# Narrower constant products on half the rows, and three more pairs of them between the projections

## The chip, the cores and the metric

The kernel runs on one core of a Trainium2 chip. The metric is the device time of one launch in microseconds (us). The time before is the median of three launches; a fourth launch was taken with the hardware profiler on, and all rows of the trace come from it.

## What is computed

Two layers on one sequence of 256 tokens with model width 2048, all in float32. The first is a hybrid layer: a norm, one wide input projection (`w_in`), a gated causal convolution, a diagonal state-space scan, two output projections that are mixed by gates, and a projection `w_o` with a residual. The second is a layer with dilated attention and an RWKV time mix side by side, an output projection, and a gated feed-forward of width 5632. Cut to the lines that matter here:

```python
m = sigmoid(ga) * ya + sigmoid(gb) * yb          # first layer: the mixture
x = rmsnorm(x + m @ w_o, final_g)                # "wo"
proj = rms_norm(x, norm1_g) @ w_in_2             # "lora", "rkv", "qkv"
mixed = concat([attention(q, k, v), rwkv(z)])
h = x + mixed @ w_out_2                          # "wouta" (attention half), "woutb" (rwkv half)
gate, up = split(rms_norm(h, norm2_g) @ w_gate_up_2)   # "ffn"
out = rms_norm(h + (silu(gate) * up) @ w_down_2, final_g_2)   # "down"
```

Batch 1, depth 1. Nothing in the change touches a value that reaches the output.

## The kernel before

Activations are kept transposed, features on the 128 partitions and the 256 tokens along the free dimension. All weights stream from memory once, as units of 128x1024 float32 (eight blocks of 128 input features for 128 output features), through a ring of four buffers. For each unit SyncE starts the load into `w_raw`, ScalarE writes the rounded copy `w_hi` (line 495), VectorE writes the remainder `w_lo` (line 976), and TensorE multiplies. The helper `unit` (lines 1680 to 1693) does it: for each of the eight blocks, three products of 128x256 into one PSUM bank, `w_hi` by the high part of the activations (line 1690), `w_hi` by the low part (line 1691) and `w_lo` by the high part (line 1692). A "column" is one block of 128 output features: two units, 48 products, where the input is 2048 wide. In the stages `glu`, `outb`, `wouta` and `woutb` a block is one unit, 24 products.

The stages follow one another in the order of `STREAM`: `u`, `zb`, `conv` (with the scan's products between its columns), `gb`, `outa`, `glu`, `outb`, `wo`, `lora`, `rkv`, `qkv` (with attention between its columns), the RWKV chunks with `wouta` between them, `woutb`, `ffn`, `down`. TensorE's program is written by hand in this order, part of it straight and part in loops (`Fori`); it waits on semaphores for `w_lo`, for a free bank, and at the start of a stage for its input. Four PSUM banks (`ps_main`) go round for the columns. The others (`ps_aux`) are used by the scan, the heads and the norms.

`half_rows` (lines 1712 to 1714) multiplies constants: twice a 64-row part of the identity (64x128) by the same rows of a ramp (64x256), each into a bank of `ps_aux` of its own. Its results are never read. It is called five times: at the start of `gb` (573 us in the trace), after the 14th block of `rkv` (1020), and after the second, third and fourth columns of `ffn` (1486, 1492, 1499). In the trace one call is four products, since a float32 product is recorded as two.

Around the new calls: `wo` runs over 16 columns in a loop of four turns, and the first column waits block by block for the mixture (`m_ready`); after each column VectorE adds the residual, makes the two parts of the next input and sums the squares (lines 1250 to 1258). `norm_total` (line 1814) sums those over partitions after half a column of `lora`. `woutb` runs over 16 blocks of one unit, with VectorE adding each into the residual (line 1604).

Of the kernel before, what the change touches and what calls it, by code (L numbers as in the profile page):

```python
# [16 lines left out]
L = 256  # L17
# [11 lines left out]
CH = 64  # L29
# [97 lines left out]
def hybrid_kernel(nc, wmain, wdown, bst_dram, cst_dram, par_dram, const_dram, x_dram, lora_dram,  # L127
                  gup_dram, bias_dram, out_dram):
    ctx = ExitStack()
    with ctx:  # L130
# [7 lines left out]
        def sem(name):  # L138
            return ctx.enter_context(nc.semaphore(name))
# [27 lines left out]
        def hilo(name, kb, blocks):  # L167
            t = wk(name, kb, [2, blocks, L], F32R)
            return t, t[:, 0, :, :], t[:, 1, :, :]
# [35 lines left out]
        ms, mh, ml = hilo("ms", 0, KB)  # L205
# [43 lines left out]
        aux = ctx.enter_context(nc.psum_tensor("ps_aux", [P, 4, 512], F32))  # L249
# [7 lines left out]
        def cst(name):  # L257
            c, w = CCOLS[name]
            return const[:, c:c + w]
# [25 lines left out]
        ya_ready, gelu_ready, yb_ready, glu_out, yo_ready, m_ready = (  # L285
            sem("ya_ready"), sem("gelu_ready"), sem("yb_ready"), sem("glu_out"), sem("yo_ready"), sem("m_ready"))
# [27 lines left out]
        def hrow(h):  # L314
            return slice(64 * h, 64 * h + 64)
# [1360 lines left out]
        def _(pe):  # L1676
# [3 lines left out]
            def unit(n, out, xs_, kb0, kbs, first, last, split=None):  # L1680

                s = n.c % RING
                high, low = xs_ if isinstance(xs_, tuple) else (xs_[:, 0, :, :], xs_[:, 1, :, :])
                pe.wait_ge(lo_ready, n.v(1))
                for kk in range(kbs):
                    w = slice(kk * P, (kk + 1) * P)
                    k = kb0 + kk
                    if split and k % (split[2:] or (1,))[0] == 0:
                        pe.wait_ge(split[0], split[1] + k // (split[2:] or (1,))[0] + 1)
                    nc.tensor.matmul(out, whi[:, s, w], high[:, k, :], start=(first and kk == 0), stop=False)  # L1690
                    nc.tensor.matmul(out, whi[:, s, w], low[:, k, :], start=False, stop=False)  # L1691
                    ins = nc.tensor.matmul(out, wlo[:, s, w], high[:, k, :], start=False, stop=(last and kk == kbs - 1))  # L1692
                ins.then_inc(unit_used, 1)

            def bank(g):
                return main[:, g.c % 4, 0:L]

            def free(g):
                if g.i is not None or g.c >= 4:
                    pe.wait_ge(bank_free[g.c % 4], g.turns(4))  # L1700

            def whole(n, out, xs_, split=None):

                unit(n, out, xs_, 0, 8, True, False, split)
                unit(n + 1, out, xs_, 8, 8, False, True, split)

            def column(n, g, xs_, split=None):

                free(g)
                whole(n, bank(g), xs_, split)  # L1710

            def half_rows(b):
                for h in range(2):
                    nc.tensor.matmul(aux[:, b + h, 0:L], cst("ident")[hrow(h), :], cst("iota")[hrow(h), :], start=True, stop=True)

            n0, g0 = UNIT0["u"], BLOCK0["u"]
            free(At(g0))
# [20 lines left out]
            n0, g0 = UNIT0["zb"], BLOCK0["zb"]  # L1738
# [30 lines left out]
            n0, g0 = UNIT0["conv"], BLOCK0["conv"]  # L1769
            with pe.Fori(0, SB) as i:  # L1770
                for p, kind in enumerate(KINDS):
# [11 lines left out]
                    else:  # L1783
                        column(n, At(g0 + conv_bank(p), 8, i), xs)
            n0, g0 = UNIT0["gb"], BLOCK0["gb"]
            half_rows(0)
            with pe.Fori(0, 4) as i:
                for b in range(4):
# [3 lines left out]
            n0, g0 = UNIT0["outa"], BLOCK0["outa"]  # L1792
# [4 lines left out]
            n0, g0 = UNIT0["glu"], BLOCK0["glu"]  # L1797
# [3 lines left out]
            n0, g0 = UNIT0["outb"], BLOCK0["outb"]  # L1801
# [2 lines left out]
                    free(At(g0 + b, 4, i))  # L1804
                    unit(At(n0 + b, 4, i), bank(At(g0 + b, 4, i)), yos, 0, 8, True, True, (yo_ready, 0) if b == 0 else None)
            n0, g0 = UNIT0["wo"], BLOCK0["wo"]
            with pe.Fori(0, 4) as i:
                for b in range(4):
                    column(At(n0 + 2 * b, 8, i), At(g0 + b, 4, i), ms, (m_ready, 0) if b == 0 else None)

            def norm_total(n, w):

# [4 lines left out]
            n0, g0 = UNIT0["lora"], BLOCK0["lora"]  # L1817
# [8 lines left out]
            n0, g0 = UNIT0["rkv"], BLOCK0["rkv"]  # L1826
# [25 lines left out]
            for b in range(12, 14):  # L1852
                column(At(n0 + 2 * b), At(g0 + b), ns)
            pe.wait_ge(kk_clamped, 1)
            half_rows(0)
            for b in range(14, 16):
                column(At(n0 + 2 * b), At(g0 + b), ns)
# [46 lines left out]
            n0 = UNIT0["qkv"]  # L1904
# [88 lines left out]
            n0 = UNIT0["wouta"]  # L1993
# [17 lines left out]
            for i in range(NCH):  # L2011
# [110 lines left out]
                if not last:  # L2122
                    wout(2)
                    for j in range(8):
                        for h in range(2):
                            ins = nc.tensor.matmul(S[hrow(h), j * CH:(j + 1) * CH], bkt[:, j, hrow(h)], st[:, j, h, :],
                                                   start=True, stop=True)
# [14 lines left out]
            n0, g0 = UNIT0["woutb"], BLOCK0["woutb"]  # L2142
            for b in range(KB):
                if b < 4 and (g0 + b) % 4 < 2:
                    pe.wait_ge(wa_free[(g0 + b) % 4], KB // 2)
                free(At(g0 + b))
                unit(At(n0 + b), bank(At(g0 + b)), (rwh, rwl), 0, 8, True, True)
            n0, g0 = UNIT0["ffn"], BLOCK0["ffn"]
            for b in range(4):
                column(At(n0 + 2 * b), At(g0 + b), x3s, (in_ready, KB) if b == 0 else None)  # L2150
                if b == 0:
                    norm_total(3, L)
                else:
                    half_rows(0)
# [3 lines left out]
            n0, g0 = UNIT0["down"], BLOCK0["down"]  # L2158
# [189 lines left out]
```

## Time and profile before

| | us |
|---|---|
| median of three launches | 2205.65 |
| the three launches | 2205.65, 2211.58, 2204.10 |
| the profiled launch | 2210.97 |
| its span, first to last instruction | 2209.3 |
| TensorE busy (matmul) | 2157.9 |
| VectorE busy | 1571.0 |
| ScalarE busy | 1042.1 |

Times of day in the rows are microseconds from the start of the span. A record of a wide product is longer than the distance to the next one, since products are pipelined and their ends are modelled; the pace is read from the starts. In the source view a row has the shortest, median and longest duration in ns, then the first and the last start. Some records of products are missing from a trace.

### The profile page before, as it was taken

The page shows a single profiled execution, that of the slowest core. Times are in us where ns is not written, and L with a number is a line of the kernel's source. Part 1 is how long each engine was busy: PE and PEld are TensorE (multiplying, and loading weights), DVE is VectorE, ACT ScalarE, POOL GpSimd, SP SyncE. Part 2 cuts the span into 40 slices and gives each one's busy share as a digit, 9 for nine tenths or more (in the row PEclk, how much of TensorE's full clock was granted, in tenths as well). Part 3 has the DMA queues.
Part 4 walks back from the last instruction along what each step waited for, and adds up shares of the span by engine and source line. Part 5 has one row for each costly group of instructions (what it writes and reads, how often), then busy time and mean ns, then how long its engine had stood idle before and what let it go on. Part 6 is the DMA issues. An engine that isn't in the chain of part 4 may idle for free.

```text
span 2209.3 us, 51676 instructions
## 1 busy us (share of the span) xinstructions
PE 2157.9 (98%) x20592; PEld 2100.5 (95%) x20592; DVE 1571.0 (71%) x2060; ACT 1042.1 (47%) x1357; POOL 267.1 (12%) x178
## 2 busy tenths in 40 slices
PE   7999999999999999999999999899999999999997
PEld 7999999999999989999999888799999999999997
DVE  7889999999645667768877767676666666654544
ACT  6544444444554444466344454564444444434443
POOL 0354544444200000100011000000000000000000
PEclk9999999999999999999999999999999999999999
DMA  7555555555665556555655111255566566666664
GB/s 260 185 172 181 181 179 180 190 184 183 196 195 195 193 191 199 180 178 172 209 185 189 62 50 41 70 181 190 190 192 195 193 194 194 190 186 196 189 191 141
DMA packets 107106, 387.84 MB, mean 176 GB/s; under 512 B 12032, under 2 KB 12160, under 8 KB 106752
## 3 DMA queue, kind: packets, MB, share of 16 engines
q1 hardware_dynamic: 104400, 375.44, 52.5%
q0 software_dynamic: 2176, 9.78, 1.3%
q8 instruction: 74, 1.21, 0.2%
q10 hardware_dynamic: 432, 1.21, 0.1%
q14 instruction: 24, 0.20, 0.0%
HBM read 384.29 MB, written 2.10 MB: 175 GB/s over the span
## 4 chain that ended last, share of the span: by engine, by line
PE 79%; DVE 14%; issue 4%; ACT 2%; DMA 0%; DVEq 0%; SPq 0%; ACTq 0%
PE ps_main L1690 23%; PE ps_main L1692 23%; PE ps_main L1691 23%; DVE w_lo L976 6%; PE ps_aux L1931 2%; ACT w_hi L495 1%; PE ps_main L1931 1%; DVE m L1135 1%; DVE m L1136 1%; PE ps_main L2004 1%; DVE acc L1142 1%; PE ps_aux L1952 1%; DMA w_raw<-wmain 0%; DVE g_scan L1145 0%; PE ps_main L2005 0%
## 5 line engine op out<-in xcount | busy, mean ns | idle before, releaser
L976 DVE TENSOR_TENSOR w_lo<-w_raw,w_hi 128x1024 fp32r<-128x1024 f32 x718 | 918.3, 1296 | 419.7 <-ACT w_hi L495 413.8
L495 ACT ACTIVATE w_hi<-w_raw 128x1024 fp32r<-128x1024 f32 x718 | 748.5, 1048 | 700.3 <-PE ps_main L1692 656.5
L1690 PE MATMUL ps_main<-xs,w_hi 128*128 128x256 f32 x1664 | 463.4, 278 | 7.2 <-DVE w_lo L976 6.1
L1691 PE MATMUL ps_main<-xs,w_hi 128*128 128x256 f32 x1664 | 460.4, 277 | 0.0
L1692 PE MATMUL ps_main<-xs,w_lo 128*128 128x256 f32 x1664 | 460.4, 277 | 0.0
L1690 PE MATMUL ps_main<-x3s,w_hi 128*128 128x256 f32 x1408 | 389.4, 277 | 0.0
L1692 PE MATMUL ps_main<-x3s,w_lo 128*128 128x256 f32 x1408 | 388.9, 276 | 0.0
L1691 PE MATMUL ps_main<-x3s,w_hi 128*128 128x256 f32 x1408 | 388.9, 276 | 0.0
L1690 PEld LDWEIGHTS ps_main<-xs,w_hi 128*128 128x128 f32 x1664 | 312.8, 188 | 15.6 <-DVE w_lo L976 11.3
L1692 PEld LDWEIGHTS ps_main<-xs,w_lo 128*128 128x128 f32 x1664 | 312.8, 188 | 0.0
L1691 PEld LDWEIGHTS ps_main<-xs,w_hi 128*128 128x128 f32 x1664 | 312.4, 188 | 0.0
L1690 PEld LDWEIGHTS ps_main<-x3s,w_hi 128*128 128x128 f32 x1408 | 264.4, 188 | 1.0 <-issue 1.0
L1692 PEld LDWEIGHTS ps_main<-x3s,w_lo 128*128 128x128 f32 x1408 | 264.4, 188 | 0.0
L1691 PEld LDWEIGHTS ps_main<-x3s,w_hi 128*128 128x128 f32 x1408 | 264.3, 188 | 0.0
L1690 PE MATMUL ps_main<-ns,w_hi 128*128 128x256 f32 x816 | 229.2, 281 | 0.3 <-DVE w_lo L976 0.3
L1692 PE MATMUL ps_main<-ns,w_lo 128*128 128x256 f32 x816 | 226.3, 277 | 0.0
L1691 PE MATMUL ps_main<-ns,w_hi 128*128 128x256 f32 x816 | 226.2, 277 | 0.0
L1690 PE MATMUL ps_main<-act,w_hi 128*128 128x256 f32 x704 | 194.3, 276 | 0.0
L1691 PE MATMUL ps_main<-act,w_hi 128*128 128x256 f32 x704 | 194.3, 276 | 0.0
L1692 PE MATMUL ps_main<-act,w_lo 128*128 128x256 f32 x704 | 194.3, 276 | 0.0
L1690 PEld LDWEIGHTS ps_main<-ns,w_hi 128*128 128x128 f32 x816 | 153.9, 189 | 7.7 <-issue 7.2
L1691 PEld LDWEIGHTS ps_main<-ns,w_hi 128*128 128x128 f32 x816 | 153.3, 188 | 0.2 <-issue 0.2
(422 smaller groups left out, 3771.5 us busy)
## 6 DMA issues: line engine op xcount, KB each, us to landing
w_raw<-wmain SPq DMA_DIRECT2D x622, 512.0 KB, 3.4
w_raw<-wdown SPq DMA_DIRECT2D x80, 512.0 KB, 3.7
w_raw<-wdown SPq DMA_DIRECT2D x16, 256.0 KB, 2.7
bias<-bias POOLq DMA_DIRECT2D x8, 384.0 KB, 3.4
x_res<-xt POOLq DMA_DIRECT2D x4, 512.0 KB, 7.0
out<-x_res SPq DMA_DIRECT2D x3, 512.0 KB, 2.8
x_first<-xt SPq DMA_DIRECT2D x2, 512.0 KB, 7.0
x_first<-xt ACTq DMA_DIRECT2D x2, 512.0 KB, 9.6
```

The costliest lines, as they stand in the source:

```text
L495: nc.scalar.activation(whi[:, s, 0:width], raw[:, s, 0:width], ACT.Copy).then_inc(hi_ready, 1)
L976: V.tensor_tensor(wlo[:, s, 0:width], raw[:, s, 0:width], whi[:, s, 0:width].bitcast(F32), ALU.subtract)\
L1135: V.tensor_tensor(m1[:, :, :], bu, cb, ALU.mult)
L1136: V.tensor_tensor(m2[:, :, :], bu, sb_, ALU.mult).then_inc(bu_used, 1)
L1142: link(V.tensor_tensor(g[:, 1, :], m1[:, 1, :], m2[:, 0, :], ALU.subtract))
L1690: nc.tensor.matmul(out, whi[:, s, w], high[:, k, :], start=(first and kk == 0), stop=False)
L1691: nc.tensor.matmul(out, whi[:, s, w], low[:, k, :], start=False, stop=False)
L1692: ins = nc.tensor.matmul(out, wlo[:, s, w], high[:, k, :], start=False, stop=(last and kk == kbs - 1))
L1931: ins = nc.tensor.matmul(banks[h][hrow(h), j * CH:(j + 1) * CH], *fn(j, h), start=True, stop=True)
L1952: ins = nc.tensor.matmul(banks[:, j // 4, (j % 4) * P:(j % 4 + 1) * P], bkc[hrow(h), j, :, :].rearrange("p a n -> p (a n)"), abr[hrow(h), ...
L2004: nc.tensor.matmul(out, whi[:, s, w], atth[:, k, :], start=(k == 0), stop=False)
```

## The change

`half_rows` multiplies only the first 64 columns of the ramp, in all its calls. It is called three times more: after the first and the second column of `wo`, and after the second block of `woutb`. For that the first four columns of `wo` are written out and the loop has three turns; the wait for the mixture stays with the first column alone.

```diff
             def half_rows(b):
                 for h in range(2):
-                    nc.tensor.matmul(aux[:, b + h, 0:L], cst("ident")[hrow(h), :], cst("iota")[hrow(h), :], start=True, stop=True)
+                    nc.tensor.matmul(aux[:, b + h, 0:CH], cst("ident")[hrow(h), :], cst("iota")[hrow(h), 0:CH],
+                                     start=True, stop=True)
...
             n0, g0 = UNIT0["wo"], BLOCK0["wo"]
-            with pe.Fori(0, 4) as i:
+            for b in range(4):
+                column(At(n0 + 2 * b), At(g0 + b), ms, (m_ready, 0) if b == 0 else None)
+                if b in (0, 1):
+                    half_rows(0)
+            with pe.Fori(1, 4) as i:
                 for b in range(4):
-                    column(At(n0 + 2 * b, 8, i), At(g0 + b, 4, i), ms, (m_ready, 0) if b == 0 else None)
+                    column(At(n0 + 2 * b, 8, i), At(g0 + b, 4, i), ms)
...
                 free(At(g0 + b))
                 unit(At(n0 + b), bank(At(g0 + b)), (rwh, rwl), 0, 8, True, True)
+                if b == 1:
+                    half_rows(0)
```

`L` is 256 and `CH` is 64.

## Rows read from the trace of the kernel before

**Rows 1.** The page: TensorE's busy time, and the granted clock in 40 slices.
```profile
PE 2157.9 (98%) x20592; PEld 2100.5 (95%) x20592; DVE 1571.0 (71%) x2060; ACT 1042.1 (47%) x1357; POOL 267.1 (12%) x178
...
PEclk9999999999999999999999999999999999999999
```

**Rows 2.** Source view, line 1690: duration ns min/median/max, first and last start.
```profile
L1690 PE MATMUL ps_main<-x3s,w_hi x1408: 276/276/468, 1474.2 to 1956.2; 128*128 128x256 f32 x176
...
L1690 PE MATMUL ps_main<-act,w_hi x704: 276/276/276, 1956.5 to 2195.5; 128*128 128x256 f32 x176
...
L1690 PE MATMUL ps_main<-yas,w_hi x256: 276/276/276, 661.4 to 748.1; 128*128 128x256 f32 x128
...
L1690 PE MATMUL ps_main<-rwkv_h,w_hi x128: 277/281/388, 1428.9 to 1473.9; 128*128 128x256 f32 x128
```

**Rows 3.** Timeline of TensorE around the pair at 1486: start, duration in us.
```profile
1485.83 0.28 PE L1692 MATMUL ps_main<-x3s,w_lo 128*128 128x256 f32 x1
1486.04 0.70 PE L1714 MATMUL ps_aux<-const 64*128 64x256 f32 x4
1486.67 0.38 PE L1690 MATMUL ps_main<-x3s,w_hi 128*128 128x256 f32 x1
1486.89 0.28 PE L1691 MATMUL ps_main<-x3s,w_hi 128*128 128x256 f32 x1
```

**Rows 4.** Source view, line 1690, in the stretches before and after each pair.
```profile
L1690 PE MATMUL ps_main<-xs,w_hi x16: 281/281/384, 567.8 to 573.2; 128*128 128x256 f32 x16
...
L1690 PE MATMUL ps_main<-xs,w_hi x256: 276/276/384, 574.3 to 661.1; 128*128 128x256 f32 x128
...
L1690 PE MATMUL ps_main<-ns,w_hi x31: 281/281/281, 1008.9 to 1019.5; 128*128 128x256 f32 x31
...
L1690 PE MATMUL ps_main<-ns,w_hi x159: 276/276/281, 1021.0 to 1074.7; 128*128 128x256 f32 x159
...
L1690 PE MATMUL ps_main<-x3s,w_hi x16: 281/281/468, 1480.1 to 1485.6; 128*128 128x256 f32 x16
...
L1690 PE MATMUL ps_main<-x3s,w_hi x16: 281/281/384, 1486.7 to 1492.1; 128*128 128x256 f32 x16
...
L1690 PE MATMUL ps_main<-x3s,w_hi x15: 276/276/281, 1493.6 to 1498.4; 128*128 128x256 f32 x15
...
L1690 PE MATMUL ps_main<-x3s,w_hi x1343: 276/276/279, 1499.9 to 1956.2; 128*128 128x256 f32 x192
```

**Rows 5.** Timeline of TensorE at the attention scores, 64-row products of two widths.
```profile
1101.77 0.50 PE L1871 MATMUL ps_main<-qkv 64*128 64x128 f32 x4
1102.09 0.61 PE L1872 MATMUL ps_main<-qkv 64*128 64x256 f32 x4
1102.63 0.38 PE L1690 MATMUL ps_main<-ns,w_hi 128*128 128x256 f32 x1
```

**Rows 6.** Start of `wo`: timeline, windows (TensorE, loads, VectorE, ScalarE, GpSimd, clock), source view.
```profile
826.31 0.42 PE L1690 MATMUL ps_main<-ms,w_hi 128*128 128x256 f32 x1 [2.20 <-DVE ms L1223]
...
826.40:829.90 3.50, 3.50 (x17) 3.48 (x18) 3.10 (x5) 1.86 (x2) 0.53 (x1) 0.52 0.78 276
...
L1690 PE MATMUL ps_main<-ms,w_hi x237: 281/281/415, 829.6 to 913.1; 128*128 128x256 f32 x119
```

**Rows 7.** Timeline of VectorE at the end of the last column of `wo`.
```profile
913.80 0.42 DVE L1250 TENSOR_TENSOR x_res<-x_res,ps_main 128x256 f32 x1 [0.44 <-PE ps_main L1692]
```

**Rows 8.** TensorE in `lora`: timeline at its two waits, source view between them.
```profile
916.75 1.13 PE L1814 MATMUL ps_aux<-acc,const 128*128 128x512 f32 x2 [0.26 <-DVE tmp L1260]
...
L1690 PE MATMUL ps_main<-ns,w_hi x42: 281/281/281, 919.8 to 934.3; 128*128 128x256 f32 x42
...
935.15 0.39 PE L1690 MATMUL ps_main<-ns,w_hi 128*128 128x256 f32 x1 [0.31 <-DVE w_lo L976]
```

**Rows 9.** Timeline of VectorE at one block of `woutb`.
```profile
1468.76 0.42 DVE L1604 TENSOR_TENSOR x_res<-x_res,ps_main 128x256 f32<-128x256 f32 x1 [0.37 <-PE ps_main L1692]
```

**Rows 10.** Before the scan's `y` products at 566.79: source view, then timeline.
```profile
L1690 PE MATMUL ps_main<-xs,w_hi x23: 276/276/276, 558.9 to 566.4; 128*128 128x256 f32 x23
...
566.79 0.41 PE L1763 MATMUL ps_aux<-h_state_a,c_stage 128*32 128x256 f32 x2
```

## The prediction

> **What bounds the kernel now.** I read the page first. TensorE is busy 98% of the span and the granted clock is full in all 40 slices [rows 1], so the time is what TensorE needs for its stream of products, not a wait for another engine. Next I read the line of the main products by operand [rows 2]. Every k-step is three wide products (128x256), and their starts give the pace. `yas`: 256 records of one line in 86.7 us, so 765 products between the first and the last, 113.3 ns each. `act`: 704 records in 239.0 us, 113.3 ns again. `rwkv_h` is the same kind of product at the same clock, and its 381 steps take 45.0 us, 117.8 ns each once the first, longer step is taken off. Nothing waits there. The reader should also see the modelled length of a record: 276 ns where the pace is 113.3, 281 ns where it is 117.8. So TensorE has two paces at full clock, 4.5 ns apart, and the 276 or 281 of a stretch tells which.
>
> When does the pace change? The same line, stretch by stretch [rows 4], says that inside an undisturbed stream it does not: 281 from 1429 to 1486, 276 for all 1343 records after 1500. It changes only at an interruption. The pair of constant products (L1714) is one. The pairs at 573, 1020 and 1492 stand between a 281 and a 276 stretch, and the pair at 1486 between two 281 stretches. The fifth, at 1499, has 276 on both sides. Of four pairs met at the slow pace three turned it, and the one met at the fast pace kept it.
>
> **The cost of a pair today.** In the timeline [rows 3] the last wide start before a pair is 1485.83 and the second after it is 1486.89: 1.06 us, where two ordinary steps at 117.8 ns take 0.24. A pair costs 0.82 us, and nothing hides it, since TensorE is the bound.
>
> **64 columns in place of 256.** No row has a 64-row, 128-column weight with 64 moving columns. The nearest are the score products [rows 5]: with 128 columns the two take 0.32 us (1101.77 to 1102.09), with 256 columns 0.54 (to 1102.63). That is 0.22 us for 128 columns, so 0.33 for the 192 that go. Bounds: nothing saved, if the weight loads set the time, and at most the 0.63 us from the pair's start to the next wide one [rows 3]. I take 0.33, since the rows are two thirds of the way there. A new pair then costs 0.49 us, and the five old ones together give back 1.65 us (0 to 3.15).
>
> The Trainium skill (TensorEngine Tiling (Array Packing), Tiling Modes, Key Properties) says that a change of tiling mode drains TensorE. That speaks against this change: the drain does not shrink with the columns, and three more pairs bring three more of them. It is inside the 0.82 us of the row here, so the sum would be the same.
>
> **The two new pairs in the mixture's projection (`wo`).** It starts at 818. TensorE waits 2.20 us for `ms`, and from 826.4 to 829.9 the granted clock is 0.52, the lower level; then it is full again and the pace is 281 to the end at 913.1 [rows 6]. The column that ends near 827.5 is the first, so the first pair falls into the slow clock and costs about double, 0.98 us. Whatever pace it leaves meets another interruption when the clock rises at 829.9, so I count no gain from it. The second pair comes a column later at full clock, 0.49 us. After it 14 columns of 48 products are left: 672 x 4.5 ns = 3.02 us if it turns the pace. VectorE does not take its place: at the end of a column it waits 0.44 us for the product [rows 7], a column shortens by 48 x 4.5 ns = 0.22 us, so 0.22 us of slack stays. Late next is the sum for the norm: TensorE already waits 0.26 us for it at 916.75 [rows 8], and that grows by the 24 x 4.5 ns of the half column before it, 0.1 us given back. The projection to the low ranks behind it is slow too (281), but it ends in a wait for `w_lo` at 935.15 [rows 8] whose chain runs over VectorE and ScalarE. I count 0 there (at most 144 x 4.5 ns = 0.65 us). Writing the first four columns out and dropping the repeated waits on `m_ready` moves no work. I put it at nothing: instructions are fetched under the stream, as in the first four columns of the feed-forward, which are written out already. Without that cover it could cost a wait of some tenths.
>
> **The pair in the second half of the output projection.** It comes after 2 of 16 blocks, 0.49 us. Left: 14 x 24 = 336 products, 1.51 us. VectorE waits 0.37 us per block for the product [rows 9], a block shortens by 0.11 us, so it stays hidden. The pace would be kept into the feed-forward, whose first three columns (to the pair at 1492) are at 281 now: 144 x 4.5 ns = 0.65 us.
>
> **Sum.** Costs: -1.65 + 0.98 + 0.49 + 0.49 = +0.31 us. Gains: -3.02 + 0.10 - 1.51 - 0.65 = -5.08 us. Together -4.8 us. The profiled execution took 2210.97 us (span 2209.3), so this would be 2206.2 under the profiler. The median of the three runs, 2205.65, lies 5.3 us below the profiled time, and the three spread over 7.5 us. That is about the size of these paces, so some of those runs may have the fast pace where the profile has the slow one. If the median run is slow in the same places it becomes 2200.9. If it is fast in all of them only +0.3 is left, 2206.0. I take 2202.6, a little nearer to the first.
>
> **The rivals.**
>
> *The pace is lost after a shorter pair* (slower). Five old calls are changed too, and the largest stretches hang on them. An interruption can also turn fast into slow: the `y` products at 566.79 stand between a 276 stretch and a 281 one [rows 10]. If a pair of another length leaves the slow pace after the third call of the feed-forward, the 84 columns left of `ffn` (4032 products) and the 2112 of `down`, 6144 in all, take 4.5 ns more: +27.6 us, 2202.6 + 27.6 = 2230. If it happens at the pair of 573, the 768 + 768 + 192 products of `gb`, `outa` and `glu` are slow: +7.8 us, 2210.4. At 1020 it is the ten columns left of `rkv`, 480 products, +2.2 us. It decides from about (6.6 + 3.0) / 0.0045 = 2100 slow products on, so by itself only in the feed-forward. For it: one of four calls failed at the slow pace. Against it: three calls in a row stand before the long stretch. The chance of the 2230 case is 0.17, of the 2210 case 0.13.
>
> *The new pairs turn nothing* (no change). They cost 0.31 us net and the slow stretches stay: 2206. The Trainium skill (TensorE: Matmul & The Clock Gate, Back-to-back issue gap) gives an isolated step as columns by clock plus a fixed floor, 109.2 ns for 256 columns, with no second pace; by it no product before a stream could change its pace. The trace differs: 113.3 and 117.8 ns in the same form. For this rival is the failed call at 1486, and that the pace may already be fast in many runs. Chance 0.2.
>
> *More than forecast*: the 64-column pair costs near nothing and turns the pace every time, and the median runs are slow as the profile is. 3.15 us saved in place of 1.65, low ranks 0.65 too, and the costs of the new pairs halved (0.98): 2200.9 - 3.1 = 2197.8. Chance 0.12.
>
> The forecast itself keeps 0.38.
>
> **How the numbers follow.** A measurement of this kernel can tell about 0.3%, 6.6 us, from no change: 2199.0 to 2212.3. Faster by more: the last rival and a tail of run spread, 0.15. Slower by more: the feed-forward case 0.17, and a third of the 2210 case, 0.04: 0.21. The rest, 0.64, is within. The range takes in the third rival from 2197.5 and the 2210 case with some spread, to 2214; it leaves out the feed-forward case (0.17) and little below.
>
> **What would show it.** In the changed profile: records of 281 or 276 ns in `ms` after the second pair, in `rwkv_h` after the pair, and in the first columns of `x3s`; a start-to-start over a pair of about 0.73 us in place of 1.06; waits for `w_lo` and for the norm's sum no more than 0.1 us longer. The prediction is wrong if the `x3s` and `act` records after the third call show 281, or if the `xs` records after 574 do, or if a pair costs as much as before. It is also wrong in its reason if the time moves with these stretches unchanged.

## The result, and the profile after

The changed kernel takes 2215.16 us (median of 18 launches, 2207.19 to 2220.59), the kernel before 2207.92 us (18 launches, 2203.10 to 2214.14). The ratio is 1.0034, with a 95% interval of 1.0024 to 1.0044: slower by 7.2 us, where 3 us less was forecast. The profiled launch took 2218.19 us with a span of 2216.5, against 2210.97 and 2209.3 before, so the two traces differ by the same 7.2 us and can be compared step by step.

The source view of line 1690 over the whole of the changed kernel answers to [rows 2]. Its columns are the durations in ns (min/median/max), then the first and last start.

```profile
L1690 PE MATMUL ps_main<-xs,w_hi x1664: 275/276/389, 60.8 to 662.8; 128*128 128x256 f32 x185
L1690 PE MATMUL ps_main<-x3s,w_hi x1408: 275/276/468, 1482.4 to 1963.4; 128*128 128x256 f32 x176
L1690 PE MATMUL ps_main<-ns,w_hi x816: 275/276/682, 917.7 to 1233.3; 128*128 128x256 f32 x164
L1690 PE MATMUL ps_main<-act,w_hi x704: 275/276/277, 1963.8 to 2202.8; 128*128 128x256 f32 x176
L1690 PE MATMUL ps_main<-yas,w_hi x256: 280/281/282, 663.1 to 753.2; 128*128 128x256 f32 x128
L1690 PE MATMUL ps_main<-ms,w_hi x256: 275/276/569, 824.3 to 917.4; 128*128 128x256 f32 x128
L1690 PE MATMUL ps_main<-yos,w_hi x128: 276/281/389, 776.2 to 823.3; 128*128 128x256 f32 x128
L1690 PE MATMUL ps_main<-rwkv_h,w_hi x128: 275/276/415, 1436.6 to 1482.1; 128*128 128x256 f32 x128
```

The row to see is `yas`: 281 ns, and 90.1 us from its first start to its last, where it was 276 ns and 86.7 us [rows 2]. `ms` and `rwkv_h`, the stages of the new pairs, read 276 in place of 281. The new pairs did not bring that. The stream was at 276 ahead of all three already, as the source view shows just before the pairs at 841.0 and 1443.9 (the one at 833.4 met 276 too):

```profile
L1690 PE MATMUL ps_main<-ms,w_hi x10: 276/276/277, 837.5 to 840.6; 128*128 128x256 f32 x10
...
L1690 PE MATMUL ps_main<-rwkv_h,w_hi x6: 276/276/277, 1441.7 to 1443.4; 128*128 128x256 f32 x6
```

The first starts of these rows, set against those of the kernel before, give where the time went:

| first start of | before | after | after less before |
|---|---|---|---|
| `xs` (`zb`) | 61.9 | 60.8 | -1.1 |
| `yas` (`outa`) | 661.4 | 663.1 | +1.7 |
| `yos` (`outb`) | 770.2 | 776.2 | +6.0 |
| `ms` (`wo`) | 818.3 | 824.3 | +6.0 |
| `ns` (`lora`) | 913.5 | 917.7 | +4.2 |
| `rwkv_h` (`woutb`) | 1428.9 | 1436.6 | +7.7 |
| `x3s` (`ffn`) | 1474.2 | 1482.4 | +8.2 |
| `act` (`down`) | 1956.5 | 1963.8 | +7.3 |
| end of the span | 2209.3 | 2216.5 | +7.2 |

From the start to `yos` +7.1 us comes in `gb`, `outa` and `glu`. `outb` is slow too (`yos` reads 281) but takes the same 48.1 us as before: TensorE waits less for `w_lo` in it, 1.3 us in place of 2.2. `wo` gives back 1.8. From `lora` to `woutb` 3.5 are lost. `woutb` gives nothing (+0.5), though its pace is the fast one.

The source view of line 1690 stretch by stretch, before and after each pair, answers to [rows 4]:

```profile
L1690 PE MATMUL ps_main<-xs,w_hi x15: 281/281/282, 566.8 to 571.8; 128*128 128x256 f32 x15
...
L1690 PE MATMUL ps_main<-xs,w_hi x255: 280/281/282, 573.0 to 662.8; 128*128 128x256 f32 x128
...
L1690 PE MATMUL ps_main<-ns,w_hi x31: 281/281/282, 1012.8 to 1023.4; 128*128 128x256 f32 x31
...
L1690 PE MATMUL ps_main<-ns,w_hi x160: 280/281/389, 1024.2 to 1080.5; 128*128 128x256 f32 x160
...
L1690 PE MATMUL ps_main<-x3s,w_hi x15: 281/281/468, 1488.1 to 1493.3; 128*128 128x256 f32 x15
...
L1690 PE MATMUL ps_main<-x3s,w_hi x16: 281/281/388, 1494.4 to 1499.8; 128*128 128x256 f32 x16
...
L1690 PE MATMUL ps_main<-x3s,w_hi x16: 276/276/387, 1500.6 to 1505.9; 128*128 128x256 f32 x16
...
L1690 PE MATMUL ps_main<-x3s,w_hi x1342: 275/276/384, 1506.7 to 1962.7; 128*128 128x256 f32 x192
```

The pairs at 572 and 1024 left the slow pace, where those of 256 columns had turned it. In the feed-forward the first failed and the second worked, as before. The two failures hold 1728 + 480 products or 7.8 + 2.2 us.

Of the 3.5 us lost between `lora` and `woutb` 2.2 are these in `rkv`. The 192 products at the start of `qkv` are fast here (276 in place of 281) and give 0.9 back. That is not luck: the 64x512 products just ahead of them (at 1075 in the kernel before) turned the pace in every one of the 14 profiles, fast to slow in the ten where `rkv` ended fast and slow to fast in the four where it ended slow. So a failed pair in `rkv` costs 1.3 us net. The rest lies behind the last `ns` product, 203.3 us to the first `rwkv_h` where the kernel before takes 200.6. It is a lower clock, the second and third of the dips below; the kernel with only the old pairs narrowed, which has no dip there, takes 200.6 as well. (A dip is a short stretch at the lower clock.) The windows view shows four dips to half, of 3.4 us each (after the window come the busy times of TensorE, its loads, VectorE, ScalarE and GpSimd, then the granted clock):

```profile
833.80:837.20 3.40, 3.40 (x18) 3.40 (x17) 3.08 (x5) 0.53 (x2) 0.00 (x0) 0.50 0.70 223
...
1253.70:1257.10 3.40, 3.38 (x70) 3.40 (x72) 0.00 (x0) 1.74 (x4) 0.00 (x0) 0.50 0.03 5
1420.90:1424.30 3.40, 3.13 (x50) 2.82 (x52) 2.04 (x3) 0.00 (x0) 0.00 (x0) 0.50 0.02 5
1438.00:1441.40 3.40, 3.40 (x19) 3.40 (x18) 2.16 (x4) 0.12 (x1) 0.00 (x0) 0.50 0.31 110
```

In the dips at 833.8 and 1438 the wide products start every 213 ns in place of 113, so 3.4 us hold 16 of them and such a dip costs about 1.6 us. The kernel before has the dip at 826 [rows 6] and one in its first 25 us. The dip at 1438 and the new pair took the gain of `woutb`: at the fast pace with neither, in the kernel with only the old pairs narrowed, the stage takes 43.6 us, and 43.6 + 1.6 + 0.6 is the 45.8 us here. Ahead of those at 833.8 and 1438 TensorE had waited, 2.26 us for `ms` and 3.2 us for `rwkv_l`. These dips come and go from launch to launch, as the experiments show.

### The profile page after: what moved, and what is told of

The parts are those of the page before. It is cut to its first block, busy times and chain, and to the rows that moved or that the text cites. A ratio compares the mean times of both kernels' runs of the same rounds, so it can differ in the third digit from the quotient of the medians.

```text
span 2216.5 us, 51686 instructions
## 1 busy us (share of the span) xinstructions
PE 2164.6 (98%) x20604; PEld 2108.0 (95%) x20604; DVE 1570.9 (71%) x2060; ACT 1041.6 (47%) x1357; POOL 267.5 (12%) x178
## 4 chain that ended last, share of the span: by engine, by line
PE 79%; DVE 14%; issue 4%; ACT 2%; DMA 1%; DVEq 0%; SPq 0%; ACTq 0%
PE ps_main L1690 24%; PE ps_main L1692 23%; PE ps_main L1691 23%; DVE w_lo L976 6%; PE ps_aux L1936 2%; PE ps_main L1936 1%; ACT w_hi L495 1%; DMA w_raw<-wmain 1%; DVE m L1135 1%; DVE m L1136 1%; PE ps_main L2009 1%; DVE acc L1142 1%; PE ps_aux L1957 1%; DVE g_scan L1145 0%; PE ps_main L2010 0%
## 5 line engine op out<-in xcount | busy, mean ns | idle before, releaser
L1690 PEld LDWEIGHTS ps_main<-ns,w_hi 128*128 128x128 f32 x816 | 153.4, 188 | 7.8 <-issue 6.8
L1692 PEld LDWEIGHTS ps_main<-ns,w_lo 128*128 128x128 f32 x816 | 153.9, 189 | 0.0
```

## The experiments

Theory A: the width. A 64-column pair turns the slow pace more rarely. Theory B: the new pairs and the dips near them cost the time, and the width is harmless. Theories C (chance, the same at every width) and D (what counts is when the stream resumes) came in with the sampling.

**The width alone.** Only the first hunk of the change, no new pair.

```diff
-                    nc.tensor.matmul(aux[:, b + h, 0:L], cst("ident")[hrow(h), :], cst("iota")[hrow(h), :], start=True, stop=True)
+                    nc.tensor.matmul(aux[:, b + h, 0:w], cst("ident")[hrow(h), :], cst("iota")[hrow(h), 0:w],
+                                     start=True, stop=True)          # w = CH
```

> The kernel before with its five pairs cut to 64 columns and no new pair. Theory A (a 64-column pair rarely turns the slow pace: 1 of 4 in the changed kernel, against 3 of 4 with 256 columns): in the profile the stretches after the pairs at the start of gb and in rkv read 281 ns, gb to glu cost 1728 x 4.5 ns = 7.8 us and rkv 2.2 us, less 5 x 0.27 us for the shorter pairs: +8 to +9 us against the kernel before, a ratio near 1.004. Theory B (the new pairs and the clock dips around them made the kernel slower, the width is harmless): -1.3 us, ratio 0.9994, with 276 ns after the two pairs.

Measured: ratio 1.0037 (1.0023 to 1.0050), 2215.85 us against 2207.98. That is as much as the whole change. Line 1690 in this kernel:

```profile
L1690 PE MATMUL ps_main<-yas,w_hi x256: 281/281/281, 664.3 to 754.4; 128*128 128x256 f32 x128
L1690 PE MATMUL ps_main<-ms,w_hi x256: 276/276/419, 825.5 to 917.4; 128*128 128x256 f32 x128
...
L1690 PE MATMUL ps_main<-rwkv_h,w_hi x128: 276/276/383, 1433.8 to 1477.0; 128*128 128x256 f32 x128
```

`yas` is slow, as theory A says. There is a second reading: `ms` and `rwkv_h` read 276 with no pair in their stages. The 281 of these stages in the kernel before [rows 2, 6] was that launch's.

**The new pairs alone, at 256 columns.** The changed kernel with `0:L` in the helper.

> All eight pairs, at 256 columns. Theory A: gb and rkv are back at 276 ns, wo after its second pair and woutb after its pair at 276 too where they were 281; three pairs cost 0.8 us each (the first 1.6 in the low clock): -5.1 + 3.2 = about -2 us, ratio 0.999, never above 1.001. Theory B: as slow as the changed kernel, ratio 1.003.

Measured: ratio 1.0007 (0.9996 to 1.0019), 2208.31 us. Theory A's forecast of 2 us less did not come either, but theory B falls. `yas`, `ms` and `rwkv_h` all read 276, and still nothing is gained over the kernel before: three pairs are paid for stages that mostly run fast anyway.

**The changed kernel with two pairs wide again**, those at the start of `gb` and in `rkv`.

```diff
-            half_rows(0)
+            half_rows(0, L)          # at the start of gb, and after the 14th column of rkv
```

> The changed kernel with only the pairs at the start of gb and in rkv back at 256 columns, the other six at 64. Theory A: both stretches at 276 ns in most launches, 8 to 10 us under the changed kernel: about -3 us against the kernel before, ratio 0.998 to 1.000. Theory B: no better than the changed kernel, 1.003.

Measured: ratio 1.0012 (1.0003 to 1.0021), 2210.35 us. Two of the eight pairs take most of the 1.0034 away. The 0.998 to 1.000 that was expected is missed. Its interval overlaps that of the version with all pairs wide. In its profile the second narrow pair of `wo`, at 834.9, failed too, so all of `wo` was slow behind it.

**No pair at `gb`.** The kernel before without the first call.

```diff
             n0, g0 = UNIT0["gb"], BLOCK0["gb"]
-            half_rows(0)
```

> The kernel before without the pair at the start of gb. If the products of gb, outa and glu keep the pace that the scan's last products left, they read 281 ns and the launch is 7.8 - 0.8 = 7 us longer, ratio 1.003. If a stream falls back to 113.3 ns by itself within it, or if the two paces are only a matter of the record, -0.8 us, ratio 0.9996.

Measured: ratio 1.0026 (1.0014 to 1.0038), 2213.78 us. The stream keeps the pace that the scan's last products left it, 281 ns for all of `gb`, `outa` and `glu`:

```profile
L1690 PE MATMUL ps_main<-xs,w_hi x270: 281/281/281, 566.8 to 661.8; 128*128 128x256 f32 x135
L1690 PE MATMUL ps_main<-yas,w_hi x256: 281/281/281, 662.2 to 752.3; 128*128 128x256 f32 x128
```

So one pair of 0.82 us was worth 5.8 us net, and the narrow one, which fails here, is worth nothing.

**Sampling the pair.** In `outa`, where columns run without a wait, each column is followed either by the scan's kind of constant products (met at 276 they left 281, in 32 of 32 samples; met at 281 they left 276, in 8 of 8) or by a pair. The pair's width is the only thing that differs between the kernels.

```diff
-            with pe.Fori(0, 4) as i:
-                for b in range(4):
-                    column(At(n0 + 2 * b, 8, i), At(g0 + b, 4, i), yas)
+            def flip():
+                for part in range(2):
+                    for t in range(TPB):
+                        nc.tensor.matmul(aux[32 * t:32 * t + 32, 2, 0:L], cst("ident")[:, 32 * t:32 * t + 32], cst("iota"),
+                                         start=(part == 0), stop=(part == 1), tile_position=(0, 32 * t))
+            for b in range(16):
+                column(At(n0 + 2 * b), At(g0 + b), yas)
+                if b % 2:
+                    half_rows(0)
+                else:
+                    flip()
```

> The kernel before with all pairs at 64 columns, and in outa, after each of its 16 columns in turn, either the scan's kind of constant products (eight of 128x32 weights by 256 columns, which turned 276 into 281 in the scan) or a pair. Each column reads 276 or 281 ns and so tells what the product before it did. Theory A (the width of a pair decides how often it turns the slow pace): at 64 columns fewer than half of the pairs met at 281 give 276; none met at 276 gives 281. Rival C (chance alone, the same for every width): about the same share as with 256 columns.

> The same with pairs of 128 columns. Theory A in its simple form (more columns, more turns) puts the share between those of 64 and 256 columns. If what counts is the moment at which the stream resumes and not the width as such (theory D), the share need not lie between. A pair should take about 0.1 us more than with 64.

> The same with pairs of 192 columns. Theory A: a share near that of 256 columns. Theory D: any share, as the resume falls 0.1 us earlier than with 256.

> The same with pairs of 256 columns, as in the kernel before. Theory A and D: nearly every pair met at 281 gives 276 (10 of 11 in the profiles so far). Rival C: no more than with 64 columns.

One launch each, 2224.99, 2225.03, 2224.24 and 2222.15 us beside 2210.46 (the sampling itself costs some 12 us). Four columns in a row with 256 columns, line 1690: after the scan's kind, after a pair, and so on.

```profile
L1690 PE MATMUL ps_main<-yas,w_hi x15: 281/281/281, 666.8 to 671.8; 128*128 128x256 f32 x15
...
L1690 PE MATMUL ps_main<-yas,w_hi x15: 276/276/281, 673.3 to 678.1; 128*128 128x256 f32 x15
...
L1690 PE MATMUL ps_main<-yas,w_hi x15: 281/281/281, 680.0 to 684.9; 128*128 128x256 f32 x15
...
L1690 PE MATMUL ps_main<-yas,w_hi x15: 276/276/281, 686.5 to 691.2; 128*128 128x256 f32 x15
```

The same with 64 columns, from the column after the second use of the scan's kind:

```profile
L1690 PE MATMUL ps_main<-yas,w_hi x15: 281/281/281, 683.0 to 688.0; 128*128 128x256 f32 x15
...
L1690 PE MATMUL ps_main<-yas,w_hi x15: 281/281/281, 689.3 to 694.2; 128*128 128x256 f32 x15
...
L1690 PE MATMUL ps_main<-yas,w_hi x15: 276/276/277, 696.1 to 700.9; 128*128 128x256 f32 x15
...
L1690 PE MATMUL ps_main<-yas,w_hi x16: 276/276/384, 701.7 to 706.9; 128*128 128x256 f32 x16
```

Here the pair at 688 leaves 281, the scan's kind turns that into 276, and the next pair keeps 276. In `outa` the pairs met at the slow pace turned it 8 times of 8 with 256 columns, 8 of 8 with 192, none of 4 with 128 and none of 4 with 64. Rival C falls. The simple form of theory A, a share that grows with the columns, falls too: it is all or nothing, with the step between 128 and 192.

The cost of each width is in the timelines around one pair, first with 64 columns, then with 128:

```profile
688.22 0.28 PE L1692 MATMUL ps_main<-yas,w_lo 128*128 128x256 f32 x1
688.42 0.44 PE L1714 MATMUL ps_aux<-const 64*128 64x64 f32 x4
688.79 0.39 PE L1690 MATMUL ps_main<-yas,w_hi 128*128 128x256 f32 x1
689.02 0.28 PE L1691 MATMUL ps_main<-yas,w_hi 128*128 128x256 f32 x1
```
```profile
671.84 0.28 PE L1692 MATMUL ps_main<-yas,w_lo 128*128 128x256 f32 x1
672.05 0.49 PE L1714 MATMUL ps_aux<-const 64*128 64x128 f32 x4
672.47 0.39 PE L1690 MATMUL ps_main<-yas,w_hi 128*128 128x256 f32 x1
672.70 0.28 PE L1691 MATMUL ps_main<-yas,w_hi 128*128 128x256 f32 x1
```

From the last wide start before to the second after: 0.80 us with 64 columns, 0.86 with 128, 0.96 with 192 and 1.06 with 256. Less two ordinary steps (0.24), a pair costs 0.56, 0.62, 0.72 and 0.82 us. From the pair's start to the next wide one it is 0.37, 0.42, 0.53 and 0.63 us.

**Two pairs in the feed-forward.** The kernel before with the first pair moved right behind the norm's product, and one less.

```diff
                 if b == 0:
                     norm_total(3, L)
-                else:
+                if b < 2:
                     half_rows(0)
```

> The kernel before with its 256-column pairs, but in the feed-forward two in place of three: one right behind the norm's product, which left 281 ns in all profiles so far, and one after the second column. If pairs of 256 turn the slow pace nearly always, the second column too reads 276 (48 x 4.5 ns = 0.2 us) and one pair's 0.8 us is saved: -1.0 us and more if the second slow column goes as well, ratio 0.9995. If two in a row are not enough, some launches are 27 us longer and the median or the highest time shows it.

Measured: ratio 1.0135 (1.0118 to 1.0152), 2235.93 us, the highest of four launches 2237.54. The main expectation, 1 us less, missed by 30 us. What it named for some launches, 27 us longer, came in all four. In its profile two 256-column pairs in a row did not turn the pace, and it stayed slow to the end of `down`. The view up to 1950:

```profile
L1690 PE MATMUL ps_main<-x3s,w_hi x1325: 281/281/281, 1482.0 to 1949.8; 128*128 128x256 f32 x190
```

All four launches were long, so this is not a rare failure but what this order does. The slow pace must then have variants that a pair answers differently. The source view of line 1692, for the one record ahead of a pair, tells them apart. First the kernel before at 1485.8 (the pair failed) and at 1492.3 (it turned):

```profile
L1692 PE MATMUL ps_main<-x3s,w_lo x1: 281/281/281, 1485.8 to 1485.8; 128*128 128x256 f32 x1
...
L1692 PE MATMUL ps_main<-x3s,w_lo x1: 279/279/279, 1492.3 to 1492.3; 128*128 128x256 f32 x1
```

The changed kernel, 64 columns, at 572.0 and 1493.8 (both failed) and, as the second record of a window, at 1500.1 (turned):

```profile
L1692 PE MATMUL ps_main<-xs,w_lo x1: 279/279/279, 572.0 to 572.0; 128*128 128x256 f32 x1
...
L1692 PE MATMUL ps_main<-x3s,w_lo x1: 279/279/279, 1493.8 to 1493.8; 128*128 128x256 f32 x1
...
L1692 PE MATMUL ps_main<-x3s,w_lo x2: 281/281/281, 1499.7 to 1500.1; 128*128 128x256 f32 x2
```

And the kernel with two pairs in the feed-forward, ahead of its second one (failed): 281 again.

```profile
L1692 PE MATMUL ps_main<-x3s,w_lo x1: 281/281/281, 1480.7 to 1480.7; 128*128 128x256 f32 x1
```

I then read this record ahead of every pair in all 14 profiles (before, after and the twelve experiments), but for three pairs in `wo` that lay in a clock dip or right at its start, and for the one right behind the norm's product in the kernel above (slow behind it):

| width of the pair | last record before it | times met | pace after it |
|---|---|---|---|
| 64 or 128 | 279 ns | 24 | slow, all 24 |
| 64 or 128 | 281 ns | 9 | fast, all 9 |
| 192, 256 or mixed | 279 ns | 46 | fast, all 46 |
| 192, 256 or mixed | 281 ns | 2 | slow, both |
| any | 276 ns (fast pace) | 34 | fast, all 34 |

No exception in 115. A pair's outcome is not chance. It goes with the variant of the slow pace that it meets and with its length. A narrow pair that fails leaves the variant that the next narrow one turns. The length was varied on purpose; the variant was only met and read off afterwards, and the row of long pairs at 281 rests on two. The next experiment tests the sentence on narrow pairs, with the outcome forecast ahead.

**A second narrow pair.** The kernel with narrow pairs, with one more a column behind the first in `gb` and in `rkv`.

```diff
+            for b in range(4):
+                if b == 2:
+                    pe.wait_ge(ga_copied, KB + GO)
+                column(At(n0 + 2 * b), At(g0 + b), xs)
+                if b == 0:
+                    half_rows(0)
-            with pe.Fori(0, 4) as i:
+            with pe.Fori(1, 4) as i:
...
             for b in range(14, 16):
                 column(At(n0 + 2 * b), At(g0 + b), ns)
+                if b == 14:
+                    half_rows(0)
```

> The kernel with five narrow pairs (64 columns), and a second narrow pair one column behind the first in gb and one column behind the first in rkv. In the feed-forward of all profiles the first narrow pair left 281 and the second, a column later, 276. If a failed pair only shifts the slow stream so that the next one turns it, gb to glu and rkv read 276 ns from their second column on: 10 us less than with one narrow pair, plus 2 x 0.57 us, about -1 us against the kernel before, ratio 0.9990 to 1.0005. If the feed-forward's order was chance, they stay at 281 and the ratio is 1.004.

Measured: ratio 1.0010 (0.9996 to 1.0024), 2207.64 us against 2205.65. Its interval and that of the narrow pairs alone (1.0023 to 1.0050) touch only at the edge, and the profile shows the expected turn, slow between the two pairs of `gb` and fast behind the second (in `rkv` the same). The 1 us less that was expected did not come:

```profile
L1690 PE MATMUL ps_main<-xs,w_hi x15: 281/281/281, 573.9 to 578.9; 128*128 128x256 f32 x15
...
L1690 PE MATMUL ps_main<-xs,w_hi x238: 276/276/276, 580.5 to 661.1; 128*128 128x256 f32 x119
```

**192 columns in the five old pairs**, `w = 192` and nothing else.

> The kernel before with its five pairs at 192 columns, which turned the slow pace 10 times of 10 and cost 0.11 us less than 256. Theory A/D: all stretches as before or better, 5 x 0.11 = 0.5 us less, ratio 0.9990 to 1.0005. If 192 columns fail in some launches, single times 8 or 27 us longer.

Measured: ratio 1.0004 (0.9994 to 1.0015), 2207.27 us, highest 2211.51. No launch failed, and the half microsecond saved is less than can be told. No version here beats the kernel before.

**Mixed widths**, the sampling kernel with 64 columns in the first product of a pair and 256 in the second.

```diff
-                    nc.tensor.matmul(aux[:, b + h, 0:w], cst("ident")[hrow(h), :], cst("iota")[hrow(h), 0:w],
+                    nc.tensor.matmul(aux[:, b + h, 0:(w, L)[h]], cst("ident")[hrow(h), :], cst("iota")[hrow(h), 0:(w, L)[h]],
```

> The kernel of the sampling runs with 64 columns in the pair's first product and 256 in the second. Theory D (what counts is how long the next wide product comes after the pair's last one: 0.20 us with 64 and 128 columns, 0.25 with 192, 0.31 with 256): the wide half sets it, 0.31 us, and nearly all eight pairs met at 281 give 276. If both halves must be wide, most stay at 281 as with 64.

One launch, 2229.18 us. All eight pairs in `outa` turned the pace, and the timeline shows the length of a full pair, 0.63 us from its start to the next wide product:

```profile
675.04 0.70 PE L1714 MATMUL ps_aux<-const 64*128 64x64 f32 x4
675.67 0.38 PE L1690 MATMUL ps_main<-yas,w_hi 128*128 128x256 f32 x1
```

The merged row hides that the halves overlap. The first record of the wide product starts 6 ns after that of the narrow one, so the wide half sets the length, and narrowing one half alone saves nothing. One wide half is enough to turn the pace. That fits theory D, but a rule that asks for one wide product would say the same. Which of the two it is stays open.

## Why the prediction was wrong

**What held.** TensorE's stream is the bound, it has two paces at full clock, and they change only at an interruption: the kernel without the pair at `gb` showed it for 1728 products. The 4.5 ns per product, the counts and the price of `gb` to `glu` (7.8 us) came out as worked out. The 2.2 us of `rkv` are 1.3 net, since `qkv` gives 0.9 back. The result is the rival "the pace is lost after a shorter pair", in its 2210 case with the `rkv` part added. For the old pairs narrowed alone this gives 7.8 + 1.3 less 5 x 0.26, or 7.8 us, and 7.9 was measured. With three new pairs at 0.56 us it gives 9.5; measured was 7.2, with an interval of 5.3 to 9.7. The rival was given 0.13. The range ended 1.2 us too low because the kernel before, with more launches, came out at 2207.92 in place of 2205.65; counted from the kernel before, the range reached to +8.4 us.

**The step that failed first: "of four pairs met at the slow pace three turned it".** I carried this count over to pairs of 64 columns and priced only their length. The turn depends on the length: where the slow stream's last record is 279 ns, which is what `gb` and `rkv` offered each time that they were slow there, a pair of 192 or more turns it and one of 64 or 128 never does. The failed one of the four was not bad luck either, it met the 281 variant. Three calls in the feed-forward are safe for both widths because the second meets the variant that the first one left. The 2230 case did not come for that reason.

**The gains of 3.02 and 1.51 us: "if it turns the pace".** There was mostly no slow pace to turn. The gains came from one profile, and that launch was not the usual one. In 10 of the 11 profiles of kernels without new pairs `wo` ran at the fast pace from the clock's rise on, and so did `woutb`. I had seen that the profiled launch lay 5.3 us above the median and still counted about half of the gain. In the changed kernel the new pairs met 276 and turned nothing. The kernel with eight wide pairs puts their worth at 1.0007 (0.9996 to 1.0019), no gain.

**"The pace would be kept into the feed-forward", 0.65 us.** The norm's product (128x256, line 1814) stands behind the first column. The changed kernel has 276 ns up to 1486.9 and 281 from 1488.1, so that product lost the pace. Every profile with wide products right behind it reads 281 there, whatever came before. I had only seen it met at the slow pace.

**The cost of a pair, mis-sized in a small way.** Narrowing saves 0.26 us and not 0.33. The step from 128 to 64 columns brings 0.05 us of the 0.26 (0.1 was expected for it), while each 64 columns above that bring 0.10. The score products could not show that, since I drew their line from 256 to 128 columns straight on. The Trainium skill (TensorEngine Tiling (Array Packing), Performance Considerations, Instruction Overhead) says that a product of one column takes as long as one of 60. No run here goes below 64, and the saving has thinned out already above it. The double price for the first pair of `wo` was not paid in the profiled launch: the pair started at 833.4, just ahead of the dip.

**The page's rule on the step.** The Trainium skill (TensorE: Matmul & The Clock Gate, Back-to-back issue gap) has one isolated gap per width. By its formula, columns by the clock plus a fixed 2.5 ns, that is 109.2 ns for 256 columns, an estimate. No run here shows it. In the streams here the same product ran at 113.3 and 117.8 ns in every kernel, and the difference decided the result.

**What stays open.** Why the slow pace exists and what its variants are is not shown, only how to read them. Why the clock dips from none to four times in a launch is open too. The numbers of dips with new pairs (four, two and three) and without (none to four) overlap, so the new pairs are not shown to cause them.

## What to carry to other kernels

An instruction whose only purpose is its effect on the pipeline's timing has no cheaper version until it is tested: here one of 0.82 us was worth 5.8 us, and one of 0.56 us at the same place was worth nothing. Before a gain is counted from a stage's pace, see it in more than one profiled launch, above all where the profiled time lies off the median. Where an outcome looks like chance, look at the record just ahead of it: 2 ns there separated all the cases.

## What was not expected of the hardware

A stream of equal 128x256 products on full weights ran at 113.3 or 117.8 ns a step at full clock, for up to 6144 products on end, and only an interruption changed it: a wait, products of another shape, or a clock dip (in the sampling kernel with 256 columns `rwkv_h` started every 118 ns just ahead of the dip at 1442.0 and every 113 behind it). The fast pace survived all 34 pairs of 64-row products. The scan's four-way products (weights 128x32) turned it over both ways, fast to slow in 32 of 32 samples and slow to fast in 8 of 8, and the 64x512 products ahead of `qkv` did so in all 14 profiles. Behind the 128x256 norm product it was always slow. A pair of 64-row products turned the slow pace or not as its length and the stream's variant went, without exception among the 81 pairs that met it, with the change between 0.42 and 0.53 us from the pair's start to the next wide product.
